# The first merge of a two-layer block: its second gate and the output projection as seven products of halves, bias rows added by VectorE

## The reference, cut to what matters

```python
h = rms_norm(x, norm_gain)
proj = h @ w_in                              # ends in merge_g, 2 x 1024 columns
y_a = (nsa_mixer(...) * silu(g_nsa)) @ w_proj_a
y_b = (rglru_mixer(...) * silu(g_lru)) @ w_proj_b
gate_a, gate_b = jnp.split(merge_g, 2, axis=-1)
m = sigmoid(gate_a) * y_a + sigmoid(gate_b) * y_b
x = x + m @ w_out                            # first output projection
```

## Time and profile before

| | |
|---|---|
| median of 3 runs | 1296.89 us |
| lowest, highest | 1291.12, 1299.49 us |
| the profiled execution's own time | 1297.56 us |
| span of its trace | 1295.8 us |
| mean granted TensorE clock | 0.981 of full speed |
| busy share of PE, DVE, ACT, POOL | 94%, 43%, 24%, 19% |

### The profile page before, as it was taken

One profiled execution on the slowest core, in us unless ns is written; L12 is line 12 of the kernel. 1 busy time (PEld: TensorE's weight loads), 2 busy tenths in 40 slices (PEclk: granted clock), 3 DMA queues, 4 the chain that ended last, 5 costly groups with the idle time before them and its releaser, 6 DMA issues.

```text
span 1295.8 us, 13572 instructions
## 1 busy us (share of the span) xinstructions
...
## 2 busy tenths in 40 slices
...
GB/s 331 167 162 249 65 1 130 65 85 144 67 178 146 98 0 147 84 95 88 108 67 129 13 53 39 95 3 65 66 116 395 167 352 393 409 400 407 410 402 179
DMA packets 94935, 212.85 MB, mean 164 GB/s; under 512 B 20109, under 2 KB 54301, under 8 KB 83047
## 3 DMA queue, kind: packets, MB, share of 16 engines
...
...
## 4 chain that ended last, share of the span: by engine, by line
PE 76%; SPq 10%; DVE 6%; DMA 3%; ACT 3%; issue 2%; ACTq 0%; POOL 0%; POOLq 0%; DVEq 0%
SPq L2860 8%; PE PS L2317 7%; PE PS L1016 6%; PE PS L642 6%; PE PS L1445 4%; PE PS L2380 4%; PE PS L1525 4%; PE PS L1708 4%; PE PS L1710 4%; PE PS L2488 3%; PE PS L2992 3%; PE PS L1454 2%; DMA AN<-in_w_down 2%; PE PS L1766 2%; PE PS L714 2%; PE PS L1754 2%
## 5 line engine op out<-in xcount | busy, mean ns | idle before, releaser
L1016 PE MATMUL PS<-HT,W 128*128 128x512 f32 x256 | 125.4, 613 | 1.8 <-ACT AN L1180 1.7
L1279 POOL TENSOR_SCALAR AN<-AN,SM 128x128 f32<-128x128 f32 (+3 forms) x64 | 72.5, 1140 | 201.8 <-DVE SM L1382 201.8
L1313 DVE SCALAR_TENSOR_TENSOR AN<-AN,COLA 128x256 f32<-128x256 f32 x168 | 86.2, 513 | 5.6 <-DMA AN<-in_w_ada 0.6
L642 PE MATMUL PS<-W,HT 128*128 128x512 f32 (+1 forms) x192 | 73.4, 541 | 0.0
L2992 PE MATMUL PS<-AN,HT 128*64 128x512 f32 x192 | 61.6, 632 | 10.6 <-DMA X<-in_w_up 6.4
L1016 PEld LDWEIGHTS PS<-HT,W 128*128 128x128 f32 x256 | 44.9, 195 | 39.4 <-issue 35.7
L3077 DVE TENSOR_TENSOR HT<-HT,PS 128x256 f32<-128x256 f32 x16 | 6.7, 422 | 130.5 <-ACT HT L3052 130.5
L1445 PE MATMUL PS<-HT,W 128*128 128x512 f32 x128 | 57.5, 597 | 0.0
L2488 PE MATMUL PS<-W,AN 128*128 128x512 f32 x128 | 57.1, 595 | 0.0
L1260 ACT ACTIVATE AN<-PS,SM 128x128 f32<-128x128 f32 (+3 forms) x64 | 33.7, 526 | 94.8 <-DVE SM L1361 94.5
L2380 PE MATMUL PS<-AN,W 128*128 128x512 f32 x128 | 55.7, 593 | 0.1
...
## 6 DMA issues: line engine op xcount, KB each, us to landing
W<-in_w_in SPq DMA_DIRECT2D x14, 2048.0 KB, 8.6
W<-in_w_down SPq DMA_DIRECT2D x20, 1024.0 KB, 27.2
AN<-in_w_gate SPq DMA_DIRECT2D x17, 1024.0 KB, 25.1
AN<-in_w_up SPq DMA_DIRECT2D x17, 1024.0 KB, 27.8
AN<-in_w_ada SPq DMA_DIRECT2D x16, 1024.0 KB, 6.0
AN<-in_w_down SPq DMA_DIRECT2D x12, 1024.0 KB, 27.1
W<-in_w_gate SPq DMA_DIRECT2D x10, 1024.0 KB, 23.0
W<-in_w_up SPq DMA_DIRECT2D x10, 1024.0 KB, 26.1
```

The costliest lines, as they stand in the source:

```text
L642: t = pe.matmul(u.ap[:, 0:nw], hT[:, c, tile(i)], wv(slot, 8, nw)[:, c, :], start=c == 0, stop=c == 7)
L1016: t = pe.matmul(u.ap, w[:, c, tile(m)], hT[:, c, :], start=c == 0, stop=c == 7)
L1279: pool.tensor_scalar(PU[u % 5][:, 0:n], PU[u % 5][:, 0:n], RSUM[:, u:u + 1], None, ALU.mult).then_inc(*sc_pool.up(u))
L1313: dve.scalar_tensor_tensor(out=a, in0=wt[:, c, :], scalar=ca["c2"][:, c:c + 1], in1=a, op0=ALU.mult, op1=ALU.add).then_inc(*ada_dve.up(p, c))
```

## The change

Gate b and the output projection are each cut into halves of the summed dimension, of the features and of the tokens, and computed by the same scheme as `pe_half`: seven products of halves, sums and differences of the operands beforehand (names S of the weights, T of the activations), and sums of the products afterwards.

- Gate b (`pe_gate7`): 7 products x 2 pairs x 8 matmuls of 128x256. Products 1 and 2 run in steps 65 to 68 of the attention; products 6, 5, 7, 4 and 3 follow as a block, then all of branch b in the order of slices 4 to 7, 0 to 3, then all of branch a. Every product waits for both W2 and W3, also those that read W2 alone.
- T of gate b is made by GpSimd before the attention (`pool_gate7`, four operations of 128x1024) in the place of x, so x is fetched again later (`x_again`, four transfers, 2 MB). S of gate b is made when W3 is there (`pool_gate7_weights`, four operations of 128x2048).
- The output projection (`pe_out7`) has 7 products x 2 token tiles x 4 matmuls of 128x512. GpSimd makes S1, S2 and S3 (128x2048 each) after the last product of branch b, T1 after slice 3 of MT1, T2 to T4 and S4 after slice 7 (`pool_out7`).
- The bias row of a modulation part is added by VectorE at the end of its chain to one partition of the sum, and the product with one row is gone. Parts 18 to 21 now have their chains behind slices 0, 2, 4 and 6 of branch b, parts 22 and 23 behind slices 0 and 2 of branch a; their `pe_ada` stands two slices later. There are two staging places instead of four, and SyncE puts both halves of `w_out` and the 2 MB of x ahead of part 18.
- The first projection of token tile 1 (`pe_qd`) moves ahead of the last transpose.

```diff
+    quarters = [MT1[:, 4 * a:4 * a + 4, 256 * b:256 * b + 256] for a in range(2) for b in range(2)]
+    GS = [B2.rearrange("p h k -> p (h k)").rearrange("p (c n) -> p c n", c=4), GL, GN]
+    OS = [W[1][:, 2048 * x:2048 * x + 2048].rearrange("p (c n) -> p c n", c=4) for x in range(2)] + [GN]
+    OT = [a.rearrange("p (c t) -> p c t", c=4) for a in
+          (AN[:, 20992:22016], HT[:, 0:1024], HT[:, 1024:2048], HT[:, 2048:3072])]
+    OU = [rgf[:, 1024 * n:1024 * n + 1024].rearrange("p (j d) -> p j d", j=2) for n in range(2)]
...
-            p0 = 32 * (kind // 3)
-            wp.wait_ge(*bars_in.at())
-            pe.matmul(u.ap[:, 0:256], ones, a, start=True, stop=False)
-            pe.matmul(u.ap[:, 0:256], ones[p0:p0 + 1, :], BAR[p0:p0 + 1, 256 * quarter:256 * quarter + 256],
-                      start=False, stop=True).then_inc(*u.filled)
+            wp.wait_ge(*bars_dve.at(p))
+            pe.matmul(u.ap[:, 0:256], ones, a, start=True, stop=True).then_inc(*u.filled)
...
-            if step > NU:
-                pe_merge1_part(pe, wp, (0, 1, 2, 4, 5)[step - NU - 1])
-        u = B.take(0, 8, "lam")
+            if NU < step <= NU + 4:
+                pe_gate7(pe, wp, *((1, 0), (1, 1), (2, 0), (2, 1))[step - NU - 1])
+        u = B.take(6, 7, "lam")
...
+        kind, quarter = divmod(PARTS[p], 4)
+        if hi == 8 and kind in (2, 5):
+            r = slice(32 * (kind // 3), 32 * (kind // 3) + 1)
+            wd.wait_ge(*bars_in.at())
+            wd.wait_ge(*ada_dve.at(p, 7))
+            dve.tensor_tensor(a[r, :], a[r, :], BAR[r, 256 * quarter:256 * quarter + 256], ALU.add).then_inc(*bars_dve.up(p))
 
     def ada_stage(p):
-        return 0 if p < ATT_PARTS else (p - ATT_PARTS) % 4
+        return 0 if p < ATT_PARTS else 2 + p % 2
...
-            if p < ATT_PARTS + 4:
-                if s == 0:
-                    ws.wait_ge(*ada_dve.at(p - 1, 7))
-                if s == 1:
-                    ws.wait_ge(*B.use("acc", 3).out)
-                if s == 2:
-                    ws.wait_ge(*B.use("acc", 3).full)
-                if s == 3:
-                    ws.wait_ge(*max_dve.at("max", NU - 1))
+            if p == ATT_PARTS:
+                ws.wait_ge(*B.use("acc", 3).full)
+            elif p == ATT_PARTS + 1:
+                ws.wait_ge(*gate7_pool.at("S", 4))
+                ws.wait_ge(*B.use("g7", 2, 1).full)
+                sp.dma_start(wv(2, 8, 512), wsrc(A["w_out"], 0, 512)).then_inc(*ring[2].up("wo", 0))
+                ws.wait_ge(*B.use("g7", 5, 1).full)
             else:
-                ws.wait_ge(*ada_dve.at(p - 4, 7))
+                ws.wait_ge(*ada_dve.at(p - 2, 7))
             sp.dma_start(STAGE[s].rearrange("p (c n) -> p c n", c=8),
                          wada[:, :, 256 * PARTS[p]:256 * PARTS[p] + 256]).then_inc(*stage_in[s].up(p))
-        for n in range(2):
-            ws.wait_ge(*B.use("gb", 4 * n + 3).full)
-            sp.dma_start(wv(2 + n, 8, 512), wsrc(A["w_out"], 512 * n, 512)).then_inc(*ring[2 + n].up("wo", n))
-
-    def ada_step(p, half):
-
-        return 1 + (2 * (p - ATT_PARTS) + half) * 25 // (2 * (24 - ATT_PARTS))
+            if p == ATT_PARTS + 1:
+                ws.wait_ge(*B.use("g7", 4, 1).full)
+                sp.dma_start(wv(3, 8, 512), wsrc(A["w_out"], 512, 512)).then_inc(*ring[3].up("wo", 1))
+                for i in range(NT):
+                    sp.dma_start(xs[:, i, :], A["x"][0, tile(i), :]).then_inc(*x_again[i].up())
...
+        wg.wait_ge(*B.use("xT", 3, 0).out)
+        wg.wait_ge(*B.use("xT", 3, 1).out)
+        b11, b12, b21, b22 = half_t
+        for i, (a, b) in enumerate(((b12, b11), (b22, TS[0]), (b22, b12), (b21, TS[1]))):
+            step(("T", i + 1), pool.tensor_tensor(TS[i], a, b, ALU.subtract))
...
+        (a11, a12), (a21, a22) = half_rows(2), half_rows(3)
+        s1, s2, s4 = GS
+        wg.wait_ge(*ring[2].at("gb", 0))
+        wg.wait_ge(*ring[3].at("gb", 1))
+        wg.wait_ge(*max_dve.at("max", NU - 1))
+        step(("S", 1), pool.tensor_tensor(s1, a21, a22, ALU.add))
+        wg.wait_ge(*ada_dve.at(ATT_PARTS - 1, 7))
+        step(("S", 2), pool.tensor_tensor(s2, s1, a11, ALU.subtract))
+        step(("S", 3), pool.tensor_tensor(a21, a11, a21, ALU.subtract))
+        wg.wait_ge(*B.use("acc", 3).out)
+        step(("S", 4), pool.tensor_tensor(s4, a12, s2, ALU.subtract))
...
+    def pe_gate7(pe, wp, x, pair):
+
+        (a11, a12), (a21, a22) = half_rows(2), half_rows(3)
+        b11, b12, b21, b22 = half_t
+        s1, s2, s4 = GS
+        s, t, lo, hi = {1: (a11, b11, 0, 2), 2: (a12, b21, 2 + 5 * pair, 3 + 5 * pair), 6: (s2, TS[1], 3, 5), 5: (s1, TS[0], 0, 6),
+                        7: (a21, TS[2], 0, 6), 4: (a22, TS[3], 0, 6), 3: (s4, b22, 0, 6)}[x]
+        u = B.take(lo, hi, "g7", x, pair)
+        wp.wait_ge(*u.free)
+        wp.wait_ge(*ring[2].at("gb", 0))
+        wp.wait_ge(*ring[3].at("gb", 1))
+        if x in (6, 5, 7, 4):
+            wp.wait_ge(*gate7_pool.at("T", {5: 1, 6: 2, 7: 3, 4: 4}[x]))
+        if x in (6, 5, 3, 7):
+            wp.wait_ge(*gate7_pool.at("S", {6: 2, 5: 1, 3: 4, 7: 3}[x]))
+        for h in range(2):
+            for c in range(4):
+                m = pe.matmul(u.ap[:, 256 * h:256 * h + 256], s[:, c, tile(2 * pair + h)], t[:, c, :], start=c == 0, stop=c == 3)
+        m.then_inc(*u.filled)
+
...
+    ORDER_B = (4, 5, 6, 7, 0, 1, 2, 3)
+    CHAIN_B, CHAIN_A = {0: 18, 2: 19, 4: 20, 6: 21}, {0: 22, 2: 23}
+    ADA_B, ADA_A = {0: 16, 1: 17, 2: 18, 4: 19, 6: 20}, {0: 21, 2: 22, 4: 23}
...
+        for x in (6, 5, 7, 4, 3):
+            for pair in range(2):
+                pe_gate7(pe, wp, x, pair)
+            if x == 6:
                 pe_ada(pe, wp, ATT_PARTS - 1)
...
+        for n, m in enumerate(ORDER_B):
...
+            if n in ADA_B:
+                pe_ada(pe, wp, ADA_B[n])
+        for m in range(8):
...
+            if m in ADA_A:
+                pe_ada(pe, wp, ADA_A[m])
...
+        dve_gate7(dve, wd, 6)
+        dve_gate7(dve, wd, 2)
+        dve_mod(dve, wd, ATT_PARTS - 1)
+        dve_gate7(dve, wd, 5)
+        dve_ada(dve, wd, 16, 0, 8)
+        dve_gate7(dve, wd, 7)
+        dve_gate7(dve, wd, 4)
+        dve_ada(dve, wd, 17, 0, 8)
+        dve_gate7(dve, wd, 3)
+        for n, m in enumerate(ORDER_B):
+            a, q = divmod(m, 4)
+            u = B.use("pb", m)
+            wd.wait_ge(*u.full)
+            for b in range(2):
+                wd.wait_ge(*sg_act.at("gb", a, b, q // 2))
+            dve.tensor_tensor(MT1[:, m, :], u.ap, MT1[:, m, :], ALU.mult).then_inc(*u.read)
+            if n - 1 in ADA_B:
+                dve_mod(dve, wd, ADA_B[n - 1])
+            if n in CHAIN_B:
+                dve_ada(dve, wd, CHAIN_B[n], 0, 8)
+        for m in range(8):
+            half, mh = divmod(m, 4)
...
+        (a11, a12), (a21, a22) = half_rows(2), half_rows(3)
+        b11, b12, b21, b22 = quarters
+        s1, s2, s4 = OS
+        wg.wait_ge(*ring[2].at("wo", 0))
+        wg.wait_ge(*ring[3].at("wo", 1))
+        wg.wait_ge(*B.use("pb", 3).full)
+        step(("S", 1), pool.tensor_tensor(s1, a21, a22, ALU.add))
+        step(("S", 2), pool.tensor_tensor(s2, s1, a11, ALU.subtract))
+        wg.wait_ge(*B.use("g7", 3, 1).full)
+        step(("S", 3), pool.tensor_tensor(a21, a11, a21, ALU.subtract))
+        wg.wait_ge(*mt_dve.at("m", 3))
+        step(("T", 1), pool.tensor_tensor(OT[0], b12, b11, ALU.subtract))
+        wg.wait_ge(*mt_dve.at("m", 7))
+        step(("T", 2), pool.tensor_tensor(OT[1], b22, OT[0], ALU.subtract))
+        step(("T", 3), pool.tensor_tensor(OT[2], b22, b12, ALU.subtract))
+        step(("T", 4), pool.tensor_tensor(OT[3], b21, OT[1], ALU.subtract))
+        step(("S", 4), pool.tensor_tensor(s4, a12, s2, ALU.subtract))
+        for j in range(2):
+            wg.wait_ge(*x_again[2 + j].at())
+            wg.wait_ge(*B.use("wo", 6, j).out)
+            xv = xs[:, 2 + j, 0:512]
+            step(("c12", j), pool.tensor_tensor(xv, xv, OU[0][:, j, :], ALU.add))
+        for j in range(2):
+            wg.wait_ge(*B.use("wo", 7, j).out)
+            xv = xs[:, 2 + j, 512:1024]
+            step(("c22", j), pool.tensor_tensor(xv, xv, OU[1][:, j, :], ALU.add))
...
+    def pe_out7(pe, wp, x, j):
+        (a11, a12), (a21, a22) = half_rows(2), half_rows(3)
+        b11, b12, b21, b22 = quarters
+        s1, s2, s4 = OS
+        s, t = {1: (a11, b11), 2: (a12, b21), 6: (s2, OT[1]), 7: (a21, OT[2]), 4: (a22, OT[3]), 5: (s1, OT[0]), 3: (s4, b22)}[x]
+        u = B.take(0, 8, "wo", x, j)
+        wp.wait_ge(*u.free)
+        wp.wait_ge(*ring[2].at("wo", 0))
+        wp.wait_ge(*ring[3].at("wo", 1))
+        if x in (6, 5, 7, 4):
+            wp.wait_ge(*out7_pool.at("T", {5: 1, 6: 2, 7: 3, 4: 4}[x]))
+        if x in (6, 5, 3, 7):
+            wp.wait_ge(*out7_pool.at("S", {6: 2, 5: 1, 3: 4, 7: 3}[x]))
+        for c in range(4):
+            wp.wait_ge(*mt_dve.at("m", c if x == 1 else 4 + c))
```

(11 more changed lines are left out.)

256 lines of the change are left out of this document (155 added, 101 removed).

## The result

| | before | changed |
|---|---|---|
| median of 20 runs | 1297.49 us | 1302.59 us |
| lowest, highest | 1290.76, 1301.08 | 1297.01, 1314.02 |
| profiled execution's own time, span | 1297.56, 1295.8 | 1300.95, 1299.2 |
| mean granted TensorE clock | 0.981 | 0.974 |

The ratio is 1.006, 95% interval 1.0041 to 1.0078: slower by 5 to 10 us, within the 1% that was called no change. Forecast were 1300 and "same". Fourteen of the twenty executions of the changed kernel lie between 1297 and 1304 us with a mean granted clock of 0.972 to 0.977, the other six between 1309 and 1314 with 0.964 to 0.967. The chain of waits of the changed kernel, by engine, answers to the earlier trace rows: TensorE lost ten points of it, and VectorE gained seven.

A forecast was written before the change was run, and what follows sets the result against it. TensorE's own work and waits were taken to bound the kernel from the merge to the second layer. -24.1 + 10.4 + 5.6 + 10.5 + 1.0 = +3.4 us gave 1300, called no change, range 1282 to 1311.

The forecast's parts named there:

- The savings: Gate b -6.5, projection -6.9, eight bias-row products -5.0, the wait at 389.9 with its slow clock -5.7; together -24.1 us.
- C: End of branch b: GpSimd's S1 to S3 hold up chain 21, `pe_ada` 21 waits 7.0; with slow clock +10.5 us.
- D: Early: `pool_gate7` delays VectorE's chain of part 1 and, through SyncE's queue, the compression weights; +1.0 us, bounds 0 and 3.
- A: First gate b product waits for W3: TensorE idles 6.9 us, with 3.5 of slow clock +10.4 us.
- B: Part 18 lands late behind `w_out` and x: TensorE waits 2.1 us, with 3.5 of slow clock +5.6 us.
- the rival for chains 22 and 23: End of branch b: chain 22 held too, a second wait of 3.7 plus 3.5, then 4.7 more; 1312, within 0.14.
- The slow clock: Each new TensorE wait costs its length plus 3.5 us of slow clock, taken from the wait at 389.9.
- The second layer: GpSimd starts its halves later relative to TensorE, still covered, with about 2 us of margin where it had 9.
- no lockout: VectorE's chains pass GpSimd unhindered, early and at the end of branch b; both costs are 0; 1289, chance 0.16.
- W3 no wait: TensorE reaches the first gate b product later, so waiting for W3 costs 0 to 3; about 1291, chance 0.06.
- two or three waits absent: Of the waits for W3, part 18 and chain 21, two absent give 1283, all three 1273; chance 0.12.
- the slower side: GpSimd's hold on VectorE reaches one chain further; 1306 to 1315, chance 0.14, of which 0.10 above 1310.

The follow-up runs named there:

- sums in halves: Changed kernel, but GpSimd makes each of the projection's S1 to S3 in two 128x1024 operations; 1304.23 us, ratio 1.0095 against the kernel before.
- sums on VectorE: Changed kernel, but VectorE makes the projection's S1 to S3 behind slices 4, 6 and 7 of branch a; 1296.23 us, ratio 1.0013 against the kernel before.

## Why the prediction was right, and where it was off

**The savings** were forecast at 6.5 + 5.0 + 5.7 in the merge. The stage grew by 6.5 with 10.1 + 5.8 + 8.3 + 0.8 of new waits in it, so 18.5 were saved for 17.2. The projection gave 6.8 for 6.9. The parts of the 18.5 were not measured one by one.

**The sum** was +3.4 and the two traced spans differ by 3.4, but that it fits so well is luck. C came out 2.2 below its term and the savings 1.2 above theirs, D came out 3.7 above, and 0.8 ahead of the projection was in no term; the first and the last stage, which vary by themselves, gave -2.8 and +2.9. The medians of twenty differ by 5.1.

**A** was 6.96 and 3.1 (forecast 6.9 and 3.5), and its removal was shown alone.

**B** was 4.16 and 1.6 (2.1 and 3.5). The sum is right (5.8 for 5.6) by two errors against each other. The part's chain began at 438.20, 1.5 later than forecast, and product 18 needs one of two banks, whose reader, the copy of part 16 (L1338), stands behind chain 18 on VectorE. So it waited about 1 us more after the chain's end:

```profile
438.20 0.35 DVE L1316 TENSOR_SCALAR AN<-AN,COLA 128x256 f32<-128x256 f32 x1 [5.72 <-DMA AN<-in_w_ada]
438.59 3.61 DVE L1319 SCALAR_TENSOR_TENSOR AN<-AN,COLA 128x256 f32<-128x256 f32 x7
442.23 0.41 DVE L1326 TENSOR_TENSOR AN<-AN 1x256 f32<-1x256 f32 x1
442.58 0.67 DVE L1596 TENSOR_TENSOR AN<-PS,AN 128x512 f32<-128x512 f32 x1
443.18 0.40 DVE L1338 COPY GBC<-PS 128x256 f32<-128x256 f32 x1
```

**C** was 6.30 and 2.0 (7.0 and 3.5). The mechanism is shown by the sums in halves and by the sums on VectorE. The wait was reckoned with 4.7 us for a sum and half a microsecond behind each; a sum took 4.5, and the bias row ended 9.5 behind the end of branch b, not 10.4. That the price is conserved, so that whatever VectorE work stands beside S1 to S3 is caught, was in the rival for chains 22 and 23 as a thing that might come on top; in the runs it came instead of C or, with the sums in halves, in part for it.

**D** is the term that was wrong: forecast 1.0, measured 4.7 in most traces and 6.4 in three. The step was to set GpSimd's four operations, from 76.6, "beside VectorE's chain of part 1, which runs 78.0 to 81.6". In the trace before the chain of part 0 runs until 77.7, so its last links already stood beside them, and that chain is the one that a product of TensorE's wants first. I looked for the price in SyncE's queue only. The rule for C, applied to every chain within reach of `pool_gate7`, would have named this chain, but not the wait: the sums start at 73.90, when two links should be left, and two links held would be over at about 79, ahead of the 81.4 at which TensorE wants them. Four links were held, as the median of 2.4 us of the seven says too. The longest of the seven began at 72.9, 1.0 us ahead of the first sum, and ended at 76.6, behind it; VectorE's line L1319 in the changed kernel, 71 to 84.1, with the shortest, the median and the longest in ns:

```profile
L1319 DVE SCALAR_TENSOR_TENSOR AN<-AN,COLA x7: 484/2446/3665, 71.3 to 81.6; 128x256 f32<-128x256 f32 x7
```

What held that link stays open. GpSimd issues transfers there (L715), but in the kernel before it issued the same ones beside the same chain, which took 3.61.

**The slow clock** as a fixed 3.5 per wait was too much: 3.1 behind A's 6.96, 1.6 behind B's 4.16, 2.0 behind C's 6.30, 1.9 behind the early 2.78. It has no order by the length of the wait, and it varies behind one and the same wait: the two slices behind the 6.30 of product 21 took 8.29 to 9.48 in the six traces that have it.

**The second layer** kept its cover but for 1.1 us. The rival "no lockout" is out by the stretched rows, "W3 no wait" by A, and "two or three waits absent" is what the edited kernels became: forecast were 1283 and 1273 without two or three of them, and with all four gone, the early one too, 1270.32 was measured. The six long executions fall into the range of the slower side; none of them left a trace, and the two traces that there are of the changed kernel have no second held chain, which was its mechanism.
